# Sums of w_down blocks made by adding DMAs from GpSimd's queue in a one-layer decoder kernel

## The reference, cut to what matters

```python
h = rmsnorm(x, ffn_norm[l])
gate = jnp.einsum('bsd,df->bsf', h, w_gate[l])
up = jnp.einsum('bsd,df->bsf', h, w_up[l])
x = x + jnp.einsum('bsf,fd->bsd', jax.nn.silu(gate) * up, w_down[l])
return rmsnorm(x, final_norm)
```

## Time and profile before

| what | us |
|---|---|
| median of three runs | 1998.9 |
| the profiled execution, its device time | 1998.37 |
| its span in the trace | 1996.5 |
| PE busy | 1985.9 |
| DVE busy | 1615.7 |
| ACT busy | 1090.7 |
| POOL busy | 146.5 |
| mean traffic | 137 GB/s |

### The profile page before, as it was taken

How to read it: one execution, slowest core, us unless ns; L and a number is a source line. 1 busy time by engine, 2 the same in 40 slices (tenths; PEclk the granted TensorE clock), 3 DMA queues, 4 the chain that set the end, 5 groups by cost and what they waited for, 6 DMA issues and landing times.

```text
span 1996.5 us, 30319 instructions
## 1 busy us (share of the span) xinstructions
PE 1985.9 (99%) x10380; PEld 1703.5 (85%) x10380; DVE 1615.7 (81%) x2319; ACT 1090.7 (55%) x2000; POOL 146.5 (7%) x241
## 2 busy tenths in 40 slices
PE   9999999999999999999999999999999999999998
PEld 8888888888888998888888888888888888888886
DVE  5666667666766899999999999999998688687776
ACT  6455556555435655555554655555456355566643
POOL 1122222222100000000000000000000000000000
PEclk9999999999999999999999999999999999999999
DMA  8222222225234444434443434443446846546433
GB/s 300 85 75 74 74 74 75 74 69 162 75 96 138 136 138 137 137 127 138 137 137 127 141 135 136 137 134 131 137 137 220 311 132 222 175 144 226 133 120 132
DMA packets 131899, 273.88 MB, mean 137 GB/s; under 512 B 13568, under 2 KB 13600, under 8 KB 130768
## 3 DMA queue, kind: packets, MB, share of 16 engines
q1 hardware_dynamic: 119344, 233.36, 36.8%
q0 software_dynamic: 6640, 23.82, 3.0%
q10 hardware_dynamic: 5808, 15.23, 2.1%
HBM read 240.89 MB, written 31.46 MB: 136 GB/s over the span
## 4 chain that ended last, share of the span: by engine, by line
PE 98%; issue 1%; ACT 1%; DVE 1%; ACTq 0%; POOL 0%; POOLq 0%
PE bank L677 27%; PE bank L680 14%; PE bank L565 8%; PE bank L567 7%; PE bank L566 7%; PE bank L609 7%; PE bank L611 7%; PE bank L610 7%; PE bank L734 3%; PE bank L736 3%; PE bank L735 3%; PE bank L761 1%; PE bank L778 1%; PE bank L746 1%; PE bank L745 1%; PE bank L777 1%
## 5 line engine op out<-in xcount | busy, mean ns | idle before, releaser
L677 PE MATMUL bank<-s_two,t_hi 128*128 128x512 f32 x2352 | 557.3, 390 | 0.0
L677 PEld LDWEIGHTS bank<-s_two,t_hi 128*128 128x128 f32 x2352 | 433.5, 188 | 84.8
L1190 ACT ACTIVATE t_hi<-t_raw 128x1792 fp32r<-128x1792 f32 x176 | 302.5, 1720 | 360.8 <-DVE t_raw L1766 273.3
L1489 DVE TENSOR_TENSOR w_lo<-raw,w_hi 128x512 fp32r<-128x512 f32 x300 | 208.7, 697 | 222.7 <-ACT w_hi L963 221.0
L1772 DVE TENSOR_TENSOR t_lo<-t_raw,t_hi 128x1792 fp32r<-128x1792 f32 x176 | 355.5, 2020 | 18.8 <-ACT t_hi L1190 18.6
L963 ACT ACTIVATE w_hi<-raw 128x512 fp32r<-128x512 f32 x300 | 188.2, 629 | 268.5 <-PE bank L611 149.1
L680 PEld LDWEIGHTS bank<-s_two,t_lo 128*128 128x128 f32 x2352 | 298.9, 191 | 10.2 <-DVE t_lo L1772 0.3
L680 PE MATMUL bank<-s_two,t_lo 128*128 128x256 f32 x2352 | 302.3, 283 | 0.0
L1763 DVE TENSOR_TENSOR t_raw<-t_raw 128x1024 f32<-128x1024 f32 x176 | 214.9, 1221 | 17.5 <-DMA t_raw<-in_w_gu 15.0
L565 PE MATMUL bank<-h_hi,w_hi 128*128 128x512 f32 x544 | 218.9, 402 | 0.0
L567 PE MATMUL bank<-h_lo,w_hi 128*128 128x512 f32 x544 | 213.2, 392 | 0.0
(11 more groups left out here) (215 smaller groups left out, 3121.7 us busy)
## 6 DMA issues: line engine op xcount, KB each, us to landing
t_raw<-in_w_gu SPq DMA_DIRECT2D x348, 256.0 KB, 2.7
raw<-in_w_in SPq DMA_DIRECT2D x136, 256.0 KB, 2.6
raw<-in_w_down SPq DMA_DIRECT2D x112, 256.0 KB, 3.6
gu_mid<-part POOLq DMA_DIRECT2D x43, 512.0 KB, 2.9
gu_next<-gu_mid SPq DMA_DIRECT2D x36, 512.0 KB, 6.4
raw<-in_w_out SPq DMA_DIRECT2D x64, 256.0 KB, 3.1
fast_y<-in_w_down SPq DMA_DIRECT2D x24, 512.0 KB, 5.1
fast_z<-in_w_down SPq DMA_DIRECT2D x16, 512.0 KB, 4.4
```

The costliest lines, as they stand in the source:

```text
L677: mm = nc.tensor.matmul(b[:, :], t_hi[r][:, ti, q, :], both, start=d == 0 and q == 0, stop=d == DOUBLES - 1 and q == 1 and i < 4, skip_gro ...
L1190: nc.scalar.activation(t_hi[r][:, :, :, :].rearrange("p a q c -> p (a q c)"), t_raw[r][:, 1:8, :, :].rearrange("p a q c -> p (a q c)"), AC ...
L1489: nc.vector.tensor_tensor(w_lo[:, s, :], raw[:, s, :], w_hi[:, s, :].bitcast(F32), ALU.subtract).then_inc(w_lo_done, 1)
```

## The change

The sums of the weight blocks leave DVE. SP loads the first block of each sum, and GpSimd issues DMAs that add the other block, read from HBM, onto the tile in SBUF (accumulate with add). As these can only add, the signs of the scheme are turned: x = B11 + B12 for P5, then + B22 for P6, then + B21 for P4; y = B12 + B22 for P7. The signs of three activation sums and of the final joins of the seven products are turned to suit (same number and size of instructions). The semaphore f_sum_done goes; x_summed and y_summed come. Per chunk SP issues 10 quarters in place of 12, and GpSimd 8 adding DMAs of a quarter each. GpSimd's program goes through these in a fixed order: x += B12 (u = 0, 1), y += B22 (u = 0, 1), x += B22 (each behind f_lo of P5), x += B21 (each behind f_lo of P6). In chunk 0 the six quarters of chunk 1 move from s = 24 to 27 to s = 20 to 23, where load_gu of chunk 1 is issued too (s = 16 to 23).

```diff
-            if s in (24, 25):
-                load_quarter("x", raw_x, 1, s - 24, 1, 2)
-                load_quarter("y", raw_y, 1, s - 24, 1, 0)
-            if s in (26, 27):
-                load_quarter("z", raw_z, 1, s - 26, 2, 2)
+            if s in (20, 21):
+                load_quarter("x", raw_x, 1, s - 20, 1, 0)
+                load_quarter("y", raw_y, 1, s - 20, 1, 2)
+            if s in (22, 23):
+                load_quarter("z", raw_z, 1, s - 22, 2, 2)
...
-                if c == 1 and e < 2:
-                    sp.wait_ge(f_sum_done, sums_count(1, e))
-                    load_quarter("y", raw_y, 1, e, 1, 2)
...
-                    load_quarter("y", raw_y, c + 1, u, 1, 0)
+                    load_quarter("y", raw_y, c + 1, u, 1, 2)
...
-                    load_quarter("x", raw_x, c + 1, u, 1, 2)
+                    load_quarter("x", raw_x, c + 1, u, 1, 0)
...
-                if e in (24, 26):
-                    u = (e - 24) // 2
-                    sp.wait_ge(f_sum_done, sums_count(c + 1, 2 * P5 + u))
-                    load_quarter("y", raw_y, c + 1, u, 1, 2)
...
-            if p in (P5, P6, P7, P4):
-                act.wait_ge(f_sum_done, sums_count(c, j if p < P3 else j - P4 * 2 + 10))
+            if p in (P5, P6, P4):
+                act.wait_ge(x_summed[u], 16 * (3 * (c - 1) + (P5, P6, P4).index(p) + 1))
+            elif p == P7:
+                act.wait_ge(y_summed[u], 16 * c)
...
-        def f_sum(c, j):
...
-                nc.vector.tensor_tensor(x, x, y, ALU.subtract).then_inc(f_sum_done, 1)
...
+        def add_quarter(b, u, summed, c, rows, n):
+
+            row = 1024 * c + 512 * (rows - 1) + 256 * u
+            nc.gpsimd.dma_start(fast_raw[b][u][:, :, :],
+                                w_down2[row:row + 256, 512 * n:512 * (n + 1)].rearrange("(k p) c -> p k c", p=P),
+                                accum_op=ALU.add).then_inc(summed[u], 16)
+
+        for c in range(1, CHUNKS):
+            for u in range(2):
+                pool.wait_ge(raw_x[u], 16 * c)
+                add_quarter("x", u, x_summed, c, 1, 2)
+            for u in range(2):
+                pool.wait_ge(raw_y[u], 16 * (2 * (c - 1) + 1))
+                add_quarter("y", u, y_summed, c, 2, 2)
+            for u in range(2):
+                pool.wait_ge(f_lo_done, fast_count(c, 2 * P5 + u))
+                add_quarter("x", u, x_summed, c, 2, 2)
+            for u in range(2):
+                pool.wait_ge(f_lo_done, fast_count(c, 2 * P6 + u))
+                add_quarter("x", u, x_summed, c, 2, 0)
```

More of the change, by code:

```diff
@@ L289, in build @@
     raw_x, raw_y, raw_z = ([sem(f"fast_{b}_loaded{u}") for u in range(2)] for b in "xyz")
-    f_sum_done, f_hi_done, f_lo_done, f_used = sem("f_sum_done"), sem("f_hi_done"), sem("f_lo_done"), sem("f_used")
+    x_summed, y_summed = ([sem(f"fast_{b}_summed{u}") for u in range(2)] for b in "xy")
+    f_hi_done, f_lo_done, f_used = sem("f_hi_done"), sem("f_lo_done"), sem("f_used")
     a_sum_done, a_hi_done, a_lo_done = sem("a_sum_done"), sem("a_hi_done"), sem("a_lo_done")
@@ L1359, in f_high @@
             elif p == P1:
-                act.wait_ge(raw_y[u], 16 * (3 * (c - 1) + 3))
+                act.wait_ge(raw_y[u], 16 * (2 * (c - 1) + 2))
             else:
@@ L1939, in a_sums @@
                 dve.wait_ge(act_done, 8 * c + 2 * u + 6)
-                nc.vector.tensor_tensor(a_sum(j), a21, a22, ALU.add).then_inc(a_sum_done, 1)
+                nc.vector.tensor_tensor(a_sum(j), a22, a21, ALU.subtract).then_inc(a_sum_done, 1)
             elif p == P6:
                 dve.wait_ge(a_sum_done, sums_count(c, 2 * P5 + u))
-                nc.vector.tensor_tensor(a_sum(j), a_sum(j), a11, ALU.subtract).then_inc(a_sum_done, 1)
+                nc.vector.tensor_tensor(a_sum(j), a_sum(j), a11, ALU.add).then_inc(a_sum_done, 1)
             elif p == P7:
@@ L1947, in a_sums @@
                 dve.wait_ge(a_sum_done, sums_count(c, 2 * P6 + u))
-                nc.vector.tensor_tensor(a_sum(j), a12, a_sum(j), ALU.subtract).then_inc(a_sum_done, 1)
+                nc.vector.tensor_tensor(a_sum(j), a_sum(j), a12, ALU.subtract).then_inc(a_sum_done, 1)
         def f_low(c, j):
@@ L1960, in a_low, with join @@
             low_half(a_lo[r][:, :, :], a_sum(j), a_hi[r][:, :, :], a_hi_done, sums_count(c, j), a_lo_done)
-        def join(p, q, op, kept_of):
+        def join(to, p, q, op, kept_of):
             dve.wait_ge(kept, FAST_U * (CHUNKS - 2) + 2 * kept_of + 2)
-            nc.vector.tensor_tensor(m_sum[:, p, :, :], m_sum[:, p, :, :], m_sum[:, q, :, :], op).then_inc(joined, 1)
+            nc.vector.tensor_tensor(m_sum[:, to, :, :], m_sum[:, p, :, :], m_sum[:, q, :, :], op).then_inc(joined, 1)
         def add_fast(p, half, n):
@@ L2002, in down_first @@
                 if s in (26, 27):
-                    f_sum(1, s - 26)
                     a_sums(1, s - 26)
@@ L2010, in down_first @@
                 if s == 30:
-                    f_sum(1, 2)
                     a_sums(1, 2)
@@ L2043, in down @@
                     if c2 < CHUNKS:
-                        f_sum(c2, j2)
                         a_sums(c2, j2)
@@ L2050, in down @@
                 if e == 20:
-                    join(P6, P1, ALU.add, P1)
-                    join(P3, P5, ALU.add, P3)
+                    join(P6, P6, P1, ALU.subtract, P1)
+                    join(P3, P3, P5, ALU.add, P3)
                 if e == 21:
                     dve.wait_ge(joined, 2)
-                    join(P7, P6, ALU.add, P7)
-                    join(P3, P6, ALU.add, P6)
+                    join(P7, P6, P7, ALU.subtract, P7)
+                    join(P3, P6, P3, ALU.subtract, P6)
                 if e == 22:
                     dve.wait_ge(joined, 4)
-                    join(P5, P7, ALU.add, P5)
+                    join(P5, P7, P5, ALU.subtract, P5)
                     add_fast(P3, 0, 2)
@@ L2062, in down @@
                     dve.wait_ge(joined, 7)
-                    join(P7, P4, ALU.subtract, P4)
+                    join(P7, P4, P7, ALU.subtract, P4)
                     add_fast(P5, 1, 2)
@@ L2068, in down @@
                 if e == 28:
-                    join(P1, P2, ALU.add, P2)
+                    join(P1, P1, P2, ALU.add, P2)
                 if e == 29:
```

## The result

| | before | changed kernel |
|---|---|---|
| median of six runs, us | 1998.7 | 2007.8 |
| span of the profiled execution, us | 1996.5 | 2005.7 |

What follows compares the result with a forecast made beforehand. PE was taken to bound the w_down stage, busy throughout at full clock. 1998.37 - 0 (removed) + 0 (added) = 1998.4 us profiled, 1998.9 us for the median: no change, range 1997.8 to 2006.0 us.

Steps and rivals of the forecast that it cites:

- DVE's relief: w_down stage: removing 32 DVE sums frees 39 us of DVE, none on the path; credit 0.
- share of 0.84: Steady chunks: DMA engines busy 68.7 of 81.6 us with the adds, so they fit.
- place 1: Each chunk's end: second half of x may be summed until about 1692 us; lands 1684 to 1691, so no PE delay.
- 5.4 us of slack: Each chunk's end: time left between ACT's split behind f_hi and PE's use of its weights in slot 29.
- Rival A: Opening, raw loads of s = 24 to 28: pile-up as queues take turns, PE waits; +5 us, 2004 us, chance 0.17.
- place (3): Opening, from s = 20: backlog of loads meets four adds; weight load takes 10 to 15 us, charged 0.
- the second figure: Opening: a weight load takes 15 us with adds at double price, against 10 us at plain price.
- 15.3 us allowed: Opening: longest a w_down weight load may take before PE stands, 9.1 - 0.6 + 6.8 us.
- double price: Each adding quarter taken as 2 plain ones, 3.4 us of all 16 engines; gives 15 us for an opening load.

Runs made afterwards that it cites:

- e4: The changed kernel with all 32 adding DMAs left out, so the weight-block sums are made by no engine; 1998.8 us, ratio 1.0000.
- e6: The changed kernel with GpSimd's first four adding DMAs (x and y of chunk 1) turned into plain loads of the same blocks; 2003.6 us, ratio 1.0024.
- e7: The changed kernel with chunk 1's gate and up arithmetic in chunk 0 three slots later on VectorE and ScalarE; 2008.4 us, ratio 1.0047.
- e1: The changed kernel with the six first quarter loads back at s = 24 to 27 of chunk 0; 2002.1 us, ratio 1.0013.
- e3: The changed kernel with the two y adds of chunk 1 moved behind the two adds that follow f_lo of P5; 2001.9 us, ratio 1.0016.

## Why the prediction was wrong

**What held.** That DVE's relief is worth nothing (e4). That the steady chunks have room: I had a share of 0.84, the trace shows 0.77 to 0.79. That an add costs about two plain transfers: 1.8 times per packet against SP's, 2.07 times per byte against GpSimd's own (e6). The sentence cited from the Trainium skill (Collectives: The Full Stack, "The bandwidth ceiling"), about half the rate for two source reads, agrees with the 2.07. The tolerance at each chunk's end (place 1) was enough. ACT in the changed kernel:

```profile
1699.03 1.06 ACT L1363 ACTIVATE f_hi<-fast_x 128x1024 fp32r<-128x1024 f32 x1 [4.90 <-DMA fast_x<-in_w_down]
...
1779.82 1.06 ACT L1363 ACTIVATE f_hi<-fast_x 128x1024 fp32r<-128x1024 f32 x1 [4.08 <-DMA fast_x<-in_w_down]
```

The second x sum came 4.9 us after ACT was ready. Before, ACT stood there too, for 2.1 us, and began at 1687.02; with everything moved by 9.2 us that is 1696.2, so f_hi was 2.8 us late, about half of the 5.4 us of slack that I had worked out (2.0 us a chunk later), and PE did not wait. Rival A had the place and the mechanism in the main, two queues that take turns: it named waits of PE in 1595 to 1612 us, and they came at 1591 to 1601 us.

**The step that failed** is place (3) of the new waits, the opening: "I charge 0, with a cover of little or nothing at the second figure". The place was the right one to watch, and the price of 0 was wrong: its weight load took 21.6 us against the 15.3 us allowed, PE waited 6.1 us, and the clock added 3.1 us. Five things in it were off.

1. The division of the engines. In the sum I let both queues drain one common backlog at 0.37 MB/us (10 to 15 us for a load) and left the other reading, turns between the queues at 0.185 MB/us, to rival A. The trace shows turns: 727 and 706 packets, with SP's queue at 0.146 MB/us while both had work and at 0.186 MB/us over the load's 20 us. The Trainium skill (DMA: Bandwidth & Descriptors, "Queues, rings and completion order") has this as a rule, round robin by packets, and the trace agrees with it. I had a rule and a reading against each other without a row, and took the one that favoured no change.
2. The landing. Rival A adds 3 us of landing to the time in the queue; the sum of the forecast does not. With them my own double price gives 15 + 3 = 18 us, over the 15.3 us that I allowed: even without turns the working pointed at a wait of PE.
3. The backlog at the start. I began it at zero at s = 20, though the engines were at 0.97 by then; the load issued at 1568.37 us took 7.7 us already. SP's queue moved 3.71 MB while the load of 21.6 us was waiting, where rival A had 2.65 MB (3.85 less 1.2), at the average rate that A had. So its step from 17 to 21.6 us lies in the amount ahead of the load; that this was the backlog of before s = 20 was not tested by a run.
4. What else waits. I gave the slack of the w_down loads alone. The gate and up tiles stand in the same queue, and VectorE waits for them in program order, with a low part of w_down behind that wait. e7 shows that this wait is not needed for the loss; it is a second one of nearly the same size.
5. The clock. PE's wait of 5.7 us was followed by some 6 us at the 1.2 GHz level. The 3.1 us that this cost stood nowhere in the working. Rival A had +5 us in all, 4.1 us short of the measured 9.1, and these 3.1 us are most of that.

The chances were off too: with a computed 15 us against an allowed 15.3 us, 0.17 was too little for a case that a row of before (ACT's split waiting for its load) had already announced.

## What to carry to other kernels

An adding DMA took about twice the engine time of a plain one here; it is free only where the engines have that room, so look at the fullest stretch of the stage, not at its mean. When a second queue gets work during a pile-up, the two took turns packet by packet here, and the first one's rate fell from 0.37 to 0.146 MB/us at once: size the latency of its loads by half the rate or less, from the backlog that is already there, and hold the new transfers back with a wait until the urgent ones have landed. Where an engine is far from the bound (DVE at 81%, PE never waiting), taking work off it brings nothing, while what replaces that work can still hurt.

## What the runs showed of the hardware that was not expected

A short stand of PE can cost more than its length. Behind waits of 5.7 us (changed kernel), 2.0 us (e1), 2.6 us (e6) and 2.0 and 2.6 us (e7) the granted clock fell, for a few us each, to a matmul every 0.42 us in place of 0.23 us; behind one of 2.4 us in the profiled execution of e3 it did not. (The three longest executions of e3, 2003.2 to 2003.7 us, have a mean granted clock of 0.998 against 0.999 in the profiled one, so it may have fallen there.) So the length of the wait does not decide it alone; what does was not settled. The cost besides the wait was 3.1 us in the changed kernel.

Two queues with work divided the engines packet by packet, not by time or bytes: 706 and 727 packets in 11 us beside the adds, 259 and 258 in 4 us beside the plain transfers of e6. What a queue gets in time follows from what its packets cost: 67.3% for the adds with packets of 2 KB, and 62.7% for plain transfers with packets of nearly 4 KB (0.96 MB in 259). So the number of packets in the other queue sets how long a load is held up: SP's queue ran at about 0.15 MB/us beside both, and was free of it when the 576 packets of e6 were through, in place of 1088.
